# Which tile comes first: both output tiles for each input tile, whole gate tiles, and other orders of work

## What is computed

```python
for i in range(2):                                   # first block, two layers
    u = rmsnorm(x, g_mix[i]) @ w_in[i]               # q, k, v of two attentions, two gates
    y_a = stick_breaking_attention(...) @ w_br_a[i]  # 8 heads of 64
    y_b = differential_attention(...)                # 4 heads, two score maps each
    y_b = (rmsnorm(y_b, g_subln[i]) * (1 - lam_init)) @ w_br_b[i]
    x = x + (sigmoid(gate_a) * y_a + sigmoid(gate_b) * y_b) @ w_o[i]
    x = x + hierarchical_moe(rmsnorm(x, g_ffn[i]), ...)   # 32 experts, 2 per token
    x = x + (p[i] @ w_ple[i]) * sigmoid(rmsnorm(x, g_ple[i]) @ w_ple_gate[i])
h = rmsnorm(x, g_final)
# second block
h = h + 0.5 * rms_norm(swiglu(rms_norm(h, g1), w_gate, w_up, w_down), post1)   # dense layer 0
h = h + rms_norm(hybrid_mixer(rms_norm(h, g_mix2)), post_mix)   # MLA and dilated attention
h = h + 0.5 * rms_norm(swiglu(rms_norm(h, g2), w_gate, w_up, w_down), post2)   # dense layer 1
```

## Time and profile before

| what | us |
|---|---|
| three runs: lowest, median, highest | 3192.3, 3195.6, 3203.2 |
| the profiled execution, its own time | 3196.9 |
| its span, first to last instruction | 3195.2 |
| TensorE busy | 3007.1 |
| VectorE busy | 1323.8 |
| GpSimd busy | 829.4 |
| ScalarE busy | 619.5 |

### The profile page before, as it was taken

One profiled execution on the slowest core, in us unless ns is written; L12 is line 12 of the kernel. 1 busy time (PEld: TensorE's weight loads), 2 busy tenths in 40 slices (PEclk: granted clock), 3 DMA queues, 4 the chain that ended last, 5 costly groups with the idle time before them and its releaser, 6 DMA issues. The chain is left out here.

```text
span 3195.2 us, 31434 instructions
## 1 busy us (share of the span) xinstructions
PE 3007.1 (94%) x12384; PEld 1875.5 (59%) x12384; DVE 1323.8 (41%) x2188; ACT 619.5 (19%) x1009; POOL 829.4 (26%) x637
## 2 busy tenths in 40 slices
PE   8999998999899999989997999998999999799996
PEld 6854464333368544643333588885654345588885
DVE  4346543111343465431223644434444464544432
ACT  2033222111210233221112300002112341300000
POOL 5200022222132000123221154543300001345443
PEclk9999999999899999989998999998999999899998
DMA  4211123999522111149996122221211111122220
GB/s 180 79 53 40 53 86 134 387 388 386 205 79 79 53 40 53 66 142 359 381 374 258 66 93 79 93 93 66 92 72 40 66 40 53 60 86 93 79 93 27
DMA packets 80914, 412.75 MB, mean 129 GB/s; under 512 B 25792, under 2 KB 25920, under 8 KB 34176
## 3 DMA queue, kind: packets, MB, share of 16 engines
q1 hardware_dynamic: 56144, 387.67, 32.1%
q0 software_dynamic: 24624, 23.08, 2.2%
HBM read 513.41 MB, written 31.46 MB: 171 GB/s over the span
## 5 line engine op out<-in xcount | busy, mean ns | idle before, releaser
L2699 POOL TENSOR_TENSOR ATT<-ring 128x512 f32<-128x512 f32 (+1 forms) x95 | 122.4, 1289 | 1195.1 <-PE PS L956 731.4
L956 PE MATMUL PS<-G,ring 128*128 128x256 f32 x1312 | 310.3, 379 | 0.0
L956 PE MATMUL PS<-HT,ring 128*128 128x256 f32 x1216 | 283.7, 386 | 25.9 <-ACT HT L2251 15.3
L956 PE MATMUL PS<-G,ATT 128*128 128x256 f32 x1184 | 280.0, 379 | 0.0
L956 PEld LDWEIGHTS PS<-HT,ring 128*128 128x128 f32 x1216 | 234.8, 194 | 65.4 <-issue 15.4
L956 PEld LDWEIGHTS PS<-G,ring 128*128 128x128 f32 x1312 | 249.3, 190 | 33.9
L956 PEld LDWEIGHTS PS<-G,ATT 128*128 128x128 f32 x1184 | 225.0, 190 | 31.9 <-issue 1.4
L2443 ACT ACTIVATE TMP<-PS 128x256 f32<-128x256 f32 x89 | 34.2, 384 | 1059.5 <-PE PS L956 939.9
L899 PE MATMUL PS<-ring,G 128*64 128x512 f32 x1024 | 229.6, 601 | 0.0
L523 PE MATMUL PS<-HT,ring 128*128 128x512 f32 x448 | 205.1, 600 | 3.8 <-DVE G L1402 3.8
L1853 DVE TENSOR_TENSOR BIG<-PS,TMP 128x256 f32<-128x256 f32 x100 | 42.4, 424 | 359.1 <-ACT TMP L2443 357.1
(11 more groups left out here) (340 smaller groups left out, 4449.3 us busy)
## 6 DMA issues: line engine op xcount, KB each, us to landing
ring<-in_stream SPq DMA_DIRECT2D x164, 1024.0 KB, 4.8
ring<-in_experts_gu SPq DMA_DIRECT2D x128, 1024.0 KB, 8.7
ring<-in_experts_down SPq DMA_DIRECT2D x64, 1024.0 KB, 8.9
G<-expert_rows SPq DMA_DIRECT2D x8, 1024.0 KB, 8.0
h_tokens<-G POOLq DMA_DIRECT2D x2, 2048.0 KB, 7.4
XT<-in_xT SPq DMA_DIRECT2D x2, 1024.0 KB, 7.8
G<-in_pT POOLq DMA_DIRECT2D x2, 512.0 KB, 6.3
out_T<-XT SPq DMA_DIRECT2D x2, 512.0 KB, 3.6
```

What stands on the lines that cost most here:

```text
L956: mm = pe.matmul(product(g, name), x[:, k * P:(k + 1) * P], y[:, k, :], start=first and k == 0 and name in ("P1", "P2", "P3", "P5"), stop= ...
L2699: pool.tensor_tensor(a["S1"], a["A21"], a["A22"], ALU.add)\
```

## The change

Nine edits (line numbers of the changed kernel are higher by 20 to 50):

- `first_unit`: in the first unit of both layers and of the mixer each raw tile is used for both output tiles at once (`two_tiles`). In the layers the norm and token sums move into the next, quartered unit, ahead of P3. In the mixer the third tile follows in PSUM bank 5, the norm and token sums stand after its third matmul.
- In the second dense layer (`ffn(1)`) the first gate unit is plain and paired in the same way; GpSimd makes no sums for it, and the norm sum stands ahead of P3 of the next unit.
- Dilated attention: `gate_fill` makes a whole gate tile in each even step and nothing in the odd ones.
- Six of the router's eight matmuls stand ahead of the output projection's last tile.
- `TABLE_AT` is 4 instead of 6, and `gate_up(0)` stands ahead of `turn_x(1)`.
- The last branch tile comes after the sub-norm sums.
- Stick-breaking: one sigmoid ahead of the rotary step, the others behind it.
- PLE: the last three raw tiles on ScalarE ahead of their squares, in VectorE the sums of tiles 4 to 7 after the last addition.
- Dense layers' output units: both squares ahead of both scales.

```diff
@@ -408,7 +408,7 @@
         POOL_X = 3
-        TABLE_AT = 6
+        TABLE_AT = 4
         DIL_ROPES = (0, 2, 8, 10, 16, 18)
@@ -465,6 +465,27 @@
+            def two_tiles(block, banks, rhs):
+                for k in range(KD):
+                    pe.wait_ge(Q["raw_ready"], now.next("raw_ready"))
+                    mm = [pe.matmul(banks[m], block(m, k), rhs[:, k, :], start=k == 0, stop=k == KD - 1)
+                          for m in range(2)]
+                return mm
+            def first_unit():
+                w = unit().rearrange("p (k c) -> p k c", k=KD)
+                banks = []
+                for m in range(2):
+                    t = now.count("lin_ready") + m
+                    if t >= 2:
+                        pe.wait_ge(Q["lin_free"], t - 1)
+                    banks.append(PS[:, t % 2, :])
+                for mm in two_tiles(lambda m, k: w[:, k, m * P:(m + 1) * P], banks, HT):
+                    mm.then_inc(Q["lin_ready"], now.inc("lin_ready"))
+                unit_used("lin_ready")
@@ -605,7 +630,17 @@
-            def output_projection(name, src):
+            def router(L, k0, k1):
+                if k0 == 0:
+                    pe.wait_ge(Q["const_landed"], N_CONST)
+                    pe.wait_ge(Q["tile_done"], 2 * len(at["groups"]))
+                for k in range(k0, k1):
+                    pe.wait_ge(Q["raw_ready"], now.next("raw_ready"))
+                    mm = pe.matmul(PS[0:NG + NE, 4, :], WR[:, L, k, :], RX[:, k, :], start=k == 0, stop=k == KD - 1)
+                if k1 == KD:
+                    mm.then_inc(Q["lg_rows"], now.inc("lg_rows"))
+            def output_projection(name, src, between=lambda: None):
@@ -621,7 +656,11 @@
                 pe.wait_ge(Q["tile_done"], 2 * (len(at["groups"]) - 1))
-                project(unit(), KD, 256, src, "lin_ready")
+                units = {}
+                for m in range(2):
+                    project_tile(units, KD, 256, src, m)
+                    if m == 0:
+                        between()
@@ -789,7 +828,7 @@
                 attention(DA_H, score, lambda qb: (qb + 1) * P, 1, 2, values, "mx_ready", fill)
-                for m in range(len(DA_BRANCH), KD):
+                for m in range(len(DA_BRANCH), KD - 1):
                     project_tile(a, 4, 512, SBQ, m)
@@ -797,6 +836,7 @@
                         .then_inc(Q["gate_ready"], now.inc("gate_ready"))
+                project_tile(a, 4, 512, SBQ, KD - 1)
...
@@ -929,8 +964,8 @@
                 turn_x(0)
+                gate_up(0)
                 turn_x(1)
-                gate_up(0)
                 for q in range(1, NSEQ):
@@ -972,7 +1007,17 @@
                     u, g = new_item([st["unit"]]), new_group(None if i else 0)
-                    if i == 1:
+                    if f == 1 and i == 0:
+                        a = weight_blocks(w, u, 4)
+                        a = [[a["A11"], a["A12"]], [a["A21"], a["A22"]]]
+                        mm = two_tiles(lambda m, k: a[m][k // 4][:, k % 4 * P:(k % 4 + 1) * P], [PS[:, 0, :], PS[:, 1, :]],
+                                       HT)[-1]
+                        mm.then_inc(Q["unit_done"], now.inc("unit_done"))
+                        unit_used("unit_done")
+                        item_done(u)
+                        at["groups"][g]["done"] = now.count("unit_done")
+                        continue
+                    if i == 1 + f:
                         drained("gate_ready")
@@ -982,11 +1027,11 @@
                                 .then_inc(Q["sum2_ready"], now.inc("sum2_ready"))
-                        if i == 0 and name == "P5" and f == 1:
-                            norm_sum(KD, 7)
+                        if i == 1 and name == "P3" and f == 1:
+                            norm_sum(KD, 3)
                         if name == "P3":
-                            pe.wait_ge(Q["wsum_ready"], u + 1)
-                        if i == 0:
+                            pe.wait_ge(Q["wsum_ready"], sums_of(u))
+                        if i == f:
                             input_sum_wait(t0, name)
@@ -1034,21 +1079,15 @@
                 at[f"in{L}"] = (len(at["items"]), len(at["groups"]), t0)
-                w = unit().rearrange("p (k c) -> p k c", k=KD)
-                for m in range(2):
-                    ps = lin_open()
-                    for k in range(KD):
-                        if m == 0:
-                            pe.wait_ge(Q["raw_ready"], now.next("raw_ready"))
-                        mm = pe.matmul(ps, w[:, k, m * P:(m + 1) * P], HT[:, k, :], start=k == 0, stop=k == KD - 1)
-                        if m == 1 and k == 3:
-                            if L == 0:
-                                pe.wait_ge(Q["x_landed"], X_LANDED)
-                            norm_sum(KD)
-                            token_sums()
-                    mm.then_inc(Q["lin_ready"], now.inc("lin_ready"))
-                unit_used("lin_ready")
-                quartered_unit(t0, 1)
+                first_unit()
+                def layer_sums(name):
+                    if name == "P3":
+                        if L == 0:
+                            pe.wait_ge(Q["x_landed"], X_LANDED)
+                        norm_sum(KD)
+                        token_sums()
+                quartered_unit(t0, 1, layer_sums)
                 drained("lin_ready")
@@ -1081,22 +1120,18 @@
             ffn(0)
-            w = unit().rearrange("p (k c) -> p k c", k=KD)
-            for m in range(2):
-                ps = lin_open()
-                for k in range(KD):
-                    if m == 0:
-                        pe.wait_ge(Q["raw_ready"], now.next("raw_ready"))
-                    mm = pe.matmul(ps, w[:, k, m * P:(m + 1) * P], HT[:, k, :], start=k == 0, stop=k == KD - 1)
-                    if m == 1 and k == 3:
-                        norm_sum(KD)
-                mm.then_inc(Q["lin_ready"], now.inc("lin_ready"))
+            first_unit()
+            w = unit()[:, 0:KD * P].rearrange("p (k c) -> p k c", k=KD)
+            for k in range(KD):
+                mm = pe.matmul(PS[:, 5, :], w[:, k, :], HT[:, k, :], start=k == 0, stop=k == KD - 1)
+                if k == 2:
+                    norm_sum(KD)
+                    for t in range(TT):
+                        column = pe.matmul(PS[:, 7, t:t + 1], ACC[:, t * P:(t + 1) * P], ONES[:, 0:1], start=t == 0,
+                                           stop=True, skip_group_check=True)
+                    column.then_inc(Q["rtok_sum"], now.inc("rtok_sum"))
+            mm.then_inc(Q["lin_ready"], now.inc("lin_ready"))
             unit_used("lin_ready")
-            for t in range(TT):
-                mm = pe.matmul(PS[:, 7, t:t + 1], ACC[:, t * P:(t + 1) * P], ONES[:, 0:1], start=t == 0, stop=True,
-                               skip_group_check=True)
-            mm.then_inc(Q["rtok_sum"], now.inc("rtok_sum"))
-            project(unit(), KD, 128, HT, "lin_ready")
             project(unit(), KD, 256, HT, "lin_ready")
@@ -1137,7 +1172,8 @@
                     roped[t] = now.count("lin_ready")
-                project_half(gates, HT, u)
+                if u % 2 == 0:
+                    project_tile(gates, KD, 256, HT, u // 2)
             at["dil"] = now.count("lin_ready")
@@ -1501,9 +1539,11 @@
                     if j:
-                        for k in range(SB_GATE[j - 1], SB_GATE[j]):
+                        next_sigmoid()
+                    rope([DAQ[:, j, :]], COS, SIN)
+                    if j:
+                        for k in range(SB_GATE[j - 1] + 1, SB_GATE[j]):
                             next_sigmoid()
-                    rope([DAQ[:, j, :]], COS, SIN)
                     for m in range(SB_GATE[j] + 1 + (j == 0), SB_GATE[j + 1]):
@@ -1892,8 +1932,15 @@
                 for i in range(0, KF, 2):
-                    quarter_sums(g0 + i, GATED)
-                    by_rstd(GATED, "gate_scaled")
+                    if f == 1 and i == 0:
+                        v.wait_ge(Q["unit_done"], at["groups"][g0]["done"])
+                        for m in range(2):
+                            v.wait_ge(*now.prev())
+                            v.tensor_tensor(GATED[:, m * S:(m + 1) * S], PS[:, m, :], RSTD[:, :], ALU.mult)\
+                                .then_inc(Q["tile_done"], now.inc("tile_done"))
+                    else:
+                        quarter_sums(g0 + i, GATED)
+                        by_rstd(GATED, "gate_scaled")
                     hid = BIGF[:, i * S:(i + 2) * S]
@@ -1906,8 +1953,7 @@
                     for k in (2 * c, 2 * c + 1):
-                        if k:
-                            sum_square()
+                        sum_square()
@@ -2052,13 +2098,11 @@
                     ple_add(k)
-                    if k >= 2:
+                    for n in range(4, KD) if k == KD - 1 else range(max(k - 2, 0), min(k - 1, 4)):
                         if L == LAYERS - 1:
```

(48 more changed lines are left out.)

29 lines of the change are left out of this document (13 added, 16 removed).

## The result

The changed kernel takes 3213.2 us (eight runs, 3204.2 to 3215.3) against 3195.4 before (eight runs, 3190.8 to 3203.2): 1.0050 times the time before, 95% interval 1.0039 to 1.0061. It is slower by 0.5%. The profiled execution was the quickest of its eight, 3204.2 us with a span of 3202.3, so its trace holds only 7 of the 18 us.

The account below looks back on a forecast made before the run. TensorE's work (3007 of 3195 us) plus its waits, and the clock around them, were taken to bound the kernel. 37.6 us saved against 42.1 lost gave 3196.9 + 4.5 - 1.3 = 3200.1 us, range 3178 to 3216.

Parts of the forecast that it names:

- within 0.3%: Total no more than 0.3% (9.6 us) from the kernel before, between 3186 and 3205.2 us; chance 0.52.
- Dilated attention: Whole gate tiles make TensorE wait between turns for VectorE's normalisation: 29 us lost, 12 more by falls of the clock.
- Rival 2: In the dilated attention the turn's gaps don't open or are half hidden: 3151 or 3170 us, chance 0.09.
- rival 3: Clock falls at nearly each gap of the dilated stage, costing 24 to 43 us: 3212 to 3231, chance 0.16.
- Second dense layer's first unit: Plain unit starts at raw tile 0 instead of waiting 10.36 us for raw tile 3: 9.1 saved (7 to 10).
- PLE into the dense layer and its output tiles: Raw tiles 5 to 7 ahead of squares on ScalarE save 4.5 us; down projection's scale leaves the chain, 1.04 each layer.
- Stick-breaking: One sigmoid ahead of the rotary step shortens TensorE's waits at pairs 1 and 3: 5.3 us saved, 3.0 more by clock.
- Sub-norm: Last branch tile behind the differential attention's sub-norm sums delays TensorE: 0.55 us lost a layer, 1.1 in all.
- Router: Six matmuls ahead of the last output tile make the last router matmul and VectorE's routing chain end about 1.35 us later.
- Table and first expert: Earlier slot table and first expert block shorten waits for gathers: 3.2 us saved in layer 0, 2.7 in layer 1, router included.
- Rival 1: The clock holds in the dilated stage, so the 12 us lost to it go: about 3188 us, chance 0.23.
- Rival 4: Paired first units don't bring their 16 us, the low clock holding through raw tiles' pauses: 7 less, 3207, chance 0.10.

Follow-up runs that it names:

- e2_whole_tiles_alone: The kernel before with whole gate tiles in the dilated attention and nothing else: 3234.3 us, 1.013 of before.
- e3_norm_first: The changed kernel with VectorE normalising ahead of the next step's maximum in the dilated attention's odd steps: 3184.4 us, 0.9969 of before.
- e8_third_sigmoid_late: e1_half_tiles with stick-breaking gate tiles taken ahead of the third sigmoid, at the last pair made only after the differential attention: 3155.4 us, 0.9878 of before.
- e5_router_whole: e1_half_tiles with all eight router matmuls behind the last output tile, as in the kernel before: 3170.4 us, 0.9915 of before.
- e1_half_tiles: The changed kernel with the dilated attention's gates back to half a tile in each step, all other edits kept: 3169.5 us, 0.9923 of before.
- e10_take_first: e1_half_tiles with VectorE taking finished gate tiles and rotary products ahead of the next maximum in the dilated attention: 3158.0 us, 0.9886 of before.
- e4_after_again: The changed kernel run once more, with nothing altered, for a second trace: 3214.8 us.
- e1_again: e1_half_tiles run once more, unaltered, as reference for later runs: 3169.3 us, 0.9915 of before.

## Why the prediction was right, and where it was off

The time on record was 3200, the range 3178 to 3216; 3213 lies in it, near its end. The direction and the main term were right. The forecast was slower by 4.5 us, it came out slower by 18, and the case "within 0.3%" had the larger chance, 0.52, and did not come true: 1.0050 with its whole interval above 1.003.

**Against its own profiled execution the sum was off by 2.6 us** (span 3202.3 against 3195.2 is 7.1 slower, forecast 4.5). That it came this close is partly luck, since this was the quickest of eight executions; the one of the second trace is 17.7 slower in its span. Term by term, from the stage table and the first trace:

- Dilated attention: forecast 29 of waits and 12 of clock, measured 26.2 and 12.7, and 38.5 in all by `e2_whole_tiles_alone`. The waits were 12 x 1.95 = 23.4 and two of 4.2 at the values product (forecast 12 of 2.1 and two of 4.3); the small ones behind rotary pairs were five of 0.5 to 0.6, where 4.0 together was forecast. The cause is shown, not argued: `e3_norm_first` removes the wait by the order alone. The clock fell six times in the stage: behind four of the twelve 1.95 us gaps, for 3.4 us each, and at both of 4.2 us, for 6.8 each. One in three plain gaps and both long ones is what the prediction had assumed; the one in three was a guess between two measured sizes, and the three traces with these gaps give 4, 5 and 4 of 12. Rival 2 (hidden gaps) and rival 3 (a fall at each gap) both missed.
- Mixer's first unit: 7.0 forecast, 7.2 measured. Second dense layer's first unit: 9.1 forecast with 1.04 for the output tiles, together 10.6 measured.
- PLE into the dense layer and its output tiles: 4.5 + 1.04 forecast, 4.7 measured (415.0 to 410.3). The 6.24 us wait became 1.79, close to the 1.7 forecast, and the norm sum then waited 1.98 for VectorE's squares. Only 3.2 of the 4.7 are waits (12.2 us idle before, 9.0 after); the rest is the clock, and the second trace, where it was low for 5.5 us, keeps 3.0.
- Stick-breaking: 8.3 forecast with the clock, 1.3 + 2.8 measured. This is the term that was mis-sized most. At pair 1 I had allowed a few tenths of handoffs; there is a wait of 0.92 there for the gate tile, which stands behind two sigmoids. At pair 3 that wait is 3.4, longer than the old 2.57 where the prediction's sign was "smaller", and the clock fell at it in both layers. In waits alone each layer saved 0.9, where 2.65 was forecast. The step "so only 0.45 is saved" named the right successor but sized its wait too low, and that a gap of this size keeps its fall was left out. `e8_third_sigmoid_late` shows what was to be had: 6 us a layer.
- Sub-norm: 0.55 forecast, 1.0 by the wait in both layers. VectorE doesn't only have the copy in its way: it stands 6.9 us before it, for a tile that comes behind the last sum, and the four products of 0.83 start only then, where before three of them were done in the shadow of the sums.
- Router: 1.35 forecast, 2.0 and 1.8 by `e5_router_whole`, of which 1.2 are waits. Table and first expert: 5.3 and 6.5 gained up to the first expert product, 1.6 and 1.5 given back behind it (forecast 1.1), so with the router 1.7 and 3.2 where 3.2 and 2.7 were forecast.
- First units of the layers: 0 and 0.7 forecast, 1.8 and 0.9 measured. The 1.8 is one fall of the clock less in the first trace (3.4 us at the low level); in the second trace, where it falls, 0.3 is left.

**What the forecast missed is the falls of the clock at the small gaps.** The 3213 is 13 us above the 3200 on record. I took 1.3 off to get from the profile to the median, as in the kernel before; the changed kernel's profiled execution lies 9 us under its median. The second trace, of an execution near the median, shows why: the same waits, and 22 us more at the low clock. Its stages show which terms lack the 13 us. The two parts from the differential scores to the token transposes lost 5.8 and 4.4 us where sub-norm and router were forecast at 1.9 each, of which 4.4 together are waits and the other 5.8 busy time, with the clock low for 10.7 and 10.8 us where the kernel before had 3.4 and 6.8. The two stick-breaking parts gained 4.2 instead of 8.3, and the start of the first dense layer 3.0 instead of 5.5. The dilated stage is not among them: 40.3 there, against 41.

The kernel before has such scatter as well (3190.8 to 3203.2). A sum made against one trace carries the falls of that execution with it, and small gains of 2 to 3 us at gaps can be paid back there, as `e5_router_whole` has it behind the router. The eight other edits were worth 31.8 us in the changed kernel's first trace (38.9 - 7.1), and 26 in the median of `e1_half_tiles`, where the sum has 36.5. Of these eight, the runs isolate the router, the branch tile and the stick-breaking order. The terms of the first units, the expert table, the PLE tiles and the output units are read from stage lengths alone; no run takes these edits out one by one.

Rival 1, the clock holding in the stage, was wrong: the clock was at its low level for 30 of 215 us there. The Trainium skill (TensorE: Matmul & The Clock Gate, section "HAM oscillation — how this bites in real kernels") says that idle gaps re-throttle the array above a length that lies between the two kinds of gap here. The falls at both 4.2 us gaps agree with it; those behind the 1.95 us gaps don't. Rival 4, first units that bring little for the low clock, didn't happen: the paired unit of the second dense layer ran at the low clock up to 2774.8 us and still caught up, since it stood 1.10 us for the last raw tile, until 2784.3.

## What to carry to other kernels

When work that fills a gap is gathered into larger pieces, look at what the other engine does in the gap that is opened, in its program's order: here VectorE did the next step's maximum before this step's normalisation, and that cost 2 us of waiting at each of 12 places and 4.2 at two more, and at six of these 14 a fall of the clock. The small waits that the gathering was to remove went away by letting VectorE do its taking while it waits anyway, and the turns didn't wait for it. And a sum of gains at gaps has to be made twice, once in waits and once for the falls of the clock that come and go with them from one execution to the next. The two edits here that closed their gaps (`e8_third_sigmoid_late`, `e10_take_first`) gained 14 and 11 us, at least what was expected of each.

## What the runs showed of the hardware

The granted clock fell behind some gaps of 1.95 us in a stage that is otherwise dense. The three traces with whole tiles and the old order on VectorE have 12 such gaps each in the dilated stage and a fall behind 4, 5 and 4 of them, for 3.4 us each; both gaps of 4.2 us had a fall in all three, for 6.8 us each. The 524 records of the stage were busy 167.2 us before and 179.9 after. The seven traces with half tiles and the old order on VectorE have three gaps of 1.60 us each in that stage and no fall behind any of the 21. All that is low in the stage there, and in `e10_take_first`, where the one gap left inside is 0.7 us, belongs to the gap of 3.6 us ahead of it.

The length of a gap alone doesn't decide it. In the latent attention TensorE stands 0.55 us and, after four transposes, 1.21 us; the clock fell there for 3.4 us in two traces (`e4_after_again` at 2685, `e1_again` at 2641.5) and not in the first trace of the changed kernel. And one kernel with the same waits spent 163 us at the low level in one execution and 185 in another, which made 9.8 us of busy time and 10.6 of the span.
